# Seven block products for eight in the two feed-forward stages of a hybrid decoder layer, with a replanned order of work

## The chip, the cores and the metric

The kernel runs on all 8 NeuronCores of one Trainium2 chip, one batch element on each, with no traffic between them. The metric is the device time of the slowest core in microseconds. TensorE is written PE, VectorE DVE, ScalarE ACT, GpSimd POOL and SyncE SP.

## The reference, cut to what matters

Each core takes x of shape 2048 x 1024 (tokens x channels) and computes one layer:

```
x = x + 0.5 * swiglu(rmsnorm(x, ffn1_norm), ffn1_w1, ffn1_w3, ffn1_w2)
... two token mixers on rmsnorm(x), gated and merged, then an output projection
... cross-attention to 256 memory tokens
x = x + 0.5 * swiglu(rmsnorm(x, ffn2_norm), ffn2_w1, ffn2_w3, ffn2_w2)
return rmsnorm(x, final_norm)
swiglu(h, w1, w3, w2) = (silu(h @ w1) * (h @ w3)) @ w2
```

w1 and w3 are 1024 x 2816, w2 is 2816 x 1024. The hidden width 2816 is 22 blocks of 128, called m below. Inputs and output are float32.

## The kernel before, in words

**Stages.** In order of time the kernel runs the first feed-forward stage (FFN1), the mixers, their merge and output projection, the cross-attention, and the second feed-forward stage (FFN2). Matmul operands are bf16, sums are float32 in the eight PSUM banks of 128 x 512. Tokens are cut into 4 blocks tb of 512 and 16 tiles tt of 128. hT holds the normalised activations, transposed: channels on the partitions (8 chunks k of 128), tokens along the row.

**Gate and up (FFN.w13, matmuls at L733, a helper that records every group).** For each m and each tb there are two products of 128 hidden units by 512 tokens, one with w1 (the gate) and one with w3 (the up part), each 8 matmuls of 128x128 by 128x512 summed in one bank. Over both products and two token blocks that is 32 matmuls per m and pair of token blocks. ACT takes silu of the one bank into STMP, DVE multiplies it by the other bank into HID (L1031).

**Down (FFN.w2).** The 22 blocks are taken in groups of 6, 6, 5 and 5. After each group, for every token tile and each half of the 1024 output channels, 6 or 5 matmuls sum the group's share in a bank and DVE adds 0.5 times the bank to the resident X (L1049), 4 x 32 additions of 128 x 512 per stage. After the last group FFN1 normalises the tile for the mixers and writes X to DRAM (park); FFN2 does the final norm and writes the output.

**Weights** are loaded by POOL's DMA queue (W<-f_w), cast from float32 to bf16 on the way, into rings of nine slots for w1/w3 and nine for w2. x, parks, rows and transposes by DMA (L940) are on SP's queue. A norm of a tile is a Square with a sum on ACT, a small DVE and a small POOL operation, a product on DVE (HB, L936), and either eight PE transposes with one copy out of the bank (L948, L956) or a DMA transpose.

**Side work in FFN1.** Beside FFN1's matmuls run the rotary tables, the centring of w_v, the small constants, and the jobs on the memory tokens (XW weights, mem_jobs), which are tied to the products in FFN1.

**The order** is not that of the program text. Prog records every operation with its reads, writes and an estimated cost; Prog.schedule plans the order of each engine by list scheduling, priority to the longest remaining path, with 70 ns for each hand-over between engines, 1/300 ns per byte and 2500 ns for a DMA; banks of one class are handed out in the order in which the program asks for them. Each engine then executes its list in order and waits on semaphores. The planning is repeated with the times of the last plan for the DMAs (PASSES).

The softmax here doesn't subtract the row's maximum and nothing guards it: scores larger than these inputs give would overflow.

## Time and profile before

| | us |
|---|---|
| median of the 3 runs shown | 2022.11 |
| lowest and highest of them | 1789.02 and 2107.54 |
| span of the profiled execution (slowest core, core 1) | 1787.4 |
| PE busy | 1707.4 (96%) |
| DVE busy | 876.6 (49%) |
| ACT busy | 648.9 (36%) |
| POOL busy | 374.1 (21%) |

The span runs from the first to the last instruction of the slowest core. The lowest run, 1789.02, stands 1.6 us over it and is what the profiled execution is set beside here; the other two runs are far above it. Busy shares of PE are of matmuls, their ends are modelled. Of the page's 40 slices of the span, PE shows 9 tenths or more in 38.

### The profile page before, as it was taken

How to read it: one execution, taken by the hardware profiler on the slowest of the kernel's cores; microseconds unless marked ns; L12 is line 12 of the kernel's file. 1: busy time of each engine (PE TensorE's matmuls, PEld its weight loads, DVE VectorE, ACT ScalarE, POOL GpSimd, SP SyncE). 2: the span in 40 equal slices, each digit the busy share in tenths (PEclk: the TensorE clock that was granted, in tenths of full speed). 3: DMA queues.
4: the chain of work that ended last, by engine and by line, in shares of the span. 5: the costliest groups of instructions: out<-in, count | busy, mean ns of one | idle time of the engine just before them, and what ended most of it. 6: DMA issues, size and time to landing. Idle time of an engine off the chain costs nothing.

```text
span 1787.4 us, 24179 instructions; the slowest of 8 cores (1769.0 to 1787.4 us)
## 1 busy us (share of the span) xinstructions
PE 1707.4 (96%) x8344; PEld 804.7 (45%) x8344; DVE 876.6 (49%) x1289; ACT 648.9 (36%) x1002; POOL 374.1 (21%) x424
## 2 busy tenths in 40 slices
PE   6999999999999989989999999998999999999997
PEld 4444454444444444444444444443444444444443
DVE  4776523244567746465665433464552232333455
ACT  5411111111236775765677633243431101011122
POOL 2200011100124444343454443210010000000000
PEclk9999999999999999999999999998999999999999
DMA  9845366721973532222112683636170320420022
GB/s 238 152 89 137 100 104 110 129 48 36 177 169 71 119 65 48 50 41 54 37 30 51 137 207 90 175 71 90 36 118 12 59 36 1 71 36 13 13 89 95
DMA packets 98647, 152.09 MB, mean 85 GB/s; under 512 B 48224, under 2 KB 60512, under 8 KB 96480
## 3 DMA queue, kind: packets, MB, share of 16 engines
q0 software_dynamic: 25488, 62.40, 22.4%
q1 hardware_dynamic: 73040, 88.14, 17.0%
q8 instruction: 70, 1.15, 0.3%
q14 instruction: 49, 0.40, 0.1%
HBM read 168.87 MB, written 33.55 MB: 113 GB/s over the span
## 4 chain that ended last, share of the span: by engine, by line
PE 84%; DMA 6%; issue 3%; DVE 3%; ACT 2%; POOL 1%; DVEq 0%; POOLq 0%; ACTq 0%; SPq 0%
PE bank L733 81%; DMA W<-f_w 2%; DMA hT<-HB 1%; DMA XW<-w_xv 1%; DMA XW<-w_xqT 1%; DVE XC L1245 1%; PE bank L948 1%; DVE T L1323 0%; POOL MU L1279 0%; POOL QK L1326 0%; DMA X<-x 0%; ACT L749 0%; DMA XW<-w_xo 0%; DMA out<-OST 0%; DVE XC L1285 0%
## 5 line engine op out<-in xcount | busy, mean ns | idle before, releaser
L733 PE MATMUL bank<-hT,W 128*128 128x512 bf16 (+1 forms) x2880 | 620.7, 376 | 3.1 <-DVE hT L956 3.1
L733 PEld LDWEIGHTS bank<-hT,W 128*128 128x128 bf16 x2880 | 282.8, 98 | 329.8 <-issue 6.1
L749 ACT ACTIVATE STMP<-bank 128x512 f32<-128x512 f32 x176 | 104.9, 596 | 629.5 <-PE bank L733 608.7
L733 PE MATMUL bank<-W,HID 128*128 128x512 bf16 x1408 | 310.6, 379 | 1.4 <-DVE HID L1031 1.4
L1049 DVE SCALAR_TENSOR_TENSOR X<-bank,X 128x512 f32<-128x512 f32 x256 | 175.1, 689 | 202.0 <-PE bank L733 201.0
L1031 DVE TENSOR_TENSOR HID<-bank,STMP 128x512 bf16<-128x512 f32 x176 | 119.8, 689 | 272.2 <-PE bank L733 270.0
L733 PEld LDWEIGHTS bank<-W,HID 128*128 128x128 bf16 x1408 | 137.7, 98 | 165.7 <-issue 1.8
L762 POOL DMA_DIRECT2D W<-f_w x89 | 48.5, 546 | 525.5 <-PE bank L733 447.9
L749 ACT ACTIVATE JUNK<-X 128x1024 bf16<-128x1024 f32 x80 | 84.5, 1056 | 141.7 <-DVE X L1049 63.2
L928 POOL TENSOR_TENSOR stat<-stat,cst 128x1 f32<-128x1 f32 x82 | 49.4, 604 | 367.9 <-DVE stat L927 362.8
L733 PE MATMUL bank<-hT,RW 128*128 128x512 bf16 x512 | 118.4, 382 | 1.6 <-DVE T L1323 0.7
L733 PE MATMUL bank<-hT,GW 128*128 128x512 bf16 x512 | 116.7, 379 | 2.9 <-DVE SC L1375 1.5
L733 PE MATMUL bank<-hT,LW 128*128 128x512 bf16 x512 | 116.2, 382 | 0.5 <-DVE SG L1336 0.5
L936 DVE SCALAR_TENSOR_TENSOR HB<-X,stat,ROW 128x1024 bf16<-128x1024 f32 x64 | 81.9, 1282 | 50.7 <-POOL stat L928 36.4
L1245 DVE SCALAR_TENSOR_TENSOR XC<-XL,pc,XC 128x1024 f32<-128x1024 f32 x48 | 65.5, 1364 | 43.1 <-ACT XL L749 41.4
L1543 DVE SCALAR_TENSOR_TENSOR TT<-TT,bank 128x512 f32<-128x512 f32 x64 | 43.8, 687 | 79.9 <-PE bank L733 75.9
L733 PEld LDWEIGHTS bank<-hT,LW 128*128 128x128 bf16 x512 | 50.3, 98 | 61.8 <-issue 2.9
L733 PEld LDWEIGHTS bank<-hT,RW 128*128 128x128 bf16 x512 | 49.7, 98 | 61.6 <-issue 5.4
L733 PEld LDWEIGHTS bank<-hT,GW 128*128 128x128 bf16 x512 | 49.4, 98 | 60.7 <-issue 4.4
L749 ACT ACT_TABLE_LOAD x50 | 64.2, 1283 | 17.2 <-PE bank L733 10.2
L749 ACT ACTIVATE TT<-GIN,dcol 128x512 f32<-128x512 f16 x64 | 42.8, 714 | 64.8 <-POOL MG L1547 63.2
L733 PE MATMUL bank<-ATP,TW 128*128 128x512 bf16 x256 | 62.1, 387 | 2.7 <-POOL ATP L1458 2.7
(162 smaller groups left out, 1800.5 us busy)
## 6 DMA issues: line engine op xcount, KB each, us to landing
W<-f_w POOLq DMA_DIRECT2D x43, 512.0 KB, 6.0
W<-f_w POOLq DMA_DIRECT2D x46, 256.0 KB, 5.3
X<-x SPq DMA_DIRECT2D x16, 512.0 KB, 7.2
park<-X SPq DMA_DIRECT2D x16, 512.0 KB, 3.0
gate_scr<-GU SPq DMA_DIRECT2D x64, 128.0 KB, 1.9
GIN<-gate_scr SPq DMA_DIRECT2D x8, 1024.0 KB, 6.5
X<-park SPq DMA_DIRECT2D x16, 512.0 KB, 6.2
out<-OST SPq DMA_DIRECT2D x16, 512.0 KB, 2.6
```

The lines of the kernel that those rows point to most:

```text
L733: ins = e.matmul(out_ap, l, r, start=(start and i == 0), stop=(stop and i == n - 1), skip_group_check=skip)
L749: P.add("act", lambda e: e.activation(out, in_, func, **kw), reads=reads, writes=writes, cost=act_cost(n, nap), tab=tab)
L762: P.add("pool", lambda e: e.dma_start(out=out, in_=in_), reads=reads, writes=writes, cost=600, dma=nbytes)
L928: pool(lambda e: e.tensor_tensor(s[:, 2:3], s[:, 1:2], cc(2), ALU.pow), hs + cst.hs, hs, 550)
L936: dve(lambda e: e.scalar_tensor_tensor(hb.ap, src.ap, r, row.ap, ALU.mult, ALU.mult), src.hs + rh + row.hs, hb.hs, D)
L948: ins = e.transpose(bv[:, c * 128:(c + 1) * 128], hb.ap[:, c * 128:(c + 1) * 128], identb.ap)
L1031: dve(lambda e: e.tensor_tensor(hd.ap, banks[b3][:, :], s.ap, ALU.mult), [hbk[b3]] + s.hs, hd.hs, TB)
L1049: dve(lambda e, b=b, xv=xv: e.scalar_tensor_tensor(xv.ap, banks[b][:, :], 0.5, xv.ap, ALU.mult, ALU.add), [hbk[b]] + xv.hs, xv.hs, 512)
L1245: dve(lambda e, s=s: e.scalar_tensor_tensor(xc.ap, XL.v(s, 1024).ap, pcol("conv_w", s * 8 + c), xc.ap, ALU.mult, ALU.add), xl_all.hs + xc. ...
L1543: dve(lambda e, t=t, by=by: e.scalar_tensor_tensor(t.ap, t.ap, 1.0, banks[by][:, :], ALU.add, ALU.mult), t.hs + [hbk[by]], t.hs, TB)
```

## The change

The diff does these things together.

- **Gate and up (FFN.unit)** works on a block of two by two: rows of hT in two halves of 512 channels, and two token blocks of 512; columns of the weights in gate and up. The four 4-matmul half products for each of the four results (8 products of 4 matmuls) are replaced by seven, in the form with sums of blocks: s1, s2, s3, s4 of the activations and t1 to t4 of the weights. All seven are summed in three banks (al, be, ep); bank al is read four times while it is added to. The sums of the activations (FFN.sums) are made by DVE once for each pair of token blocks; those of the weights (FFN.wsum) by DVE for m below 5 and by POOL for the others. Values are rounded to bf16 and stored as fp16, so that sums of them fit. In FFN1 the first five m on the first two token blocks stay plain (FFN.plain).
- **Evacuation**: per unit three copies and two silus on ACT, three additions and one product on DVE, one product on POOL.
- **All 22 m go before the down projection**; HID is held for all tokens, X isn't resident. The down projection sums 22 matmuls in a bank, reloads x (or the park) tile by tile from DRAM, and adds once. Four tiles share the eight banks while w2 arrives (WAVE, CHUNKS).
- **Down of FFN2 (down_blocks)**: after the first four tiles, seven products of 11 matmuls for eight, on pairs of token tiles and halves of the hidden width and of the output.
- **Weights** go through five slots (NSLOT) instead of nine; w2 is loaded whole into space that the gate and up phase gives back.
- **The memory jobs move** from FFN1 into the first five steps of the mixers (MSCHED); two gate pieces are early (EARLY); the rest of the side work stands beside FFN1's down projection.
- **The first loads** are in a written order (ORDER0), at most four under way (WIN0).
- **Attention**: the normalisation of one head's exponentials is recorded after the scores of the next.
- **The last tile** (tt 14, which comes after 15) is finished in halves (last_tile).
- **The planner** gets a latency for each pair of engines, 1/240 ns per byte and 3000 ns for a DMA, and a random addition to the priorities by seeds (SEEDS, JIT).

```diff
-SEM_NS = 70.0
-DMA_NS_PER_B = 1.0 / 300.0
-DMA_LAT = 2500.0
+DMA_NS_PER_B = 1.0 / 240.0
+DMA_LAT = 3000.0
+LAT = {("pe", "act"): 262.0, ("pe", "dve"): 272.0, ("act", "dve"): 140.0, ("dve", "act"): 95.0, ("dve", "pool"): 145.0,
+       ("act", "pool"): 145.0, ("pool", "dve"): 104.0, ("pool", "act"): 95.0}
...
-GROUPS = [6, 6, 5, 5]
...
+NSLOT = 5
+LEAD = 4
+LEAD2 = 3
+TDVE = 5
+NPLAIN = 5
+ORDER0 = "x0 r x1 w0 x2 x3 w1 x4 w2 x5 x6 x7 w3 x8 x9 w4 x10 x11 x12 x13 x14 x15"
+WIN0 = 4
+WAVE = 4
+CHUNKS = [4] + [2] * 9
...
     class FFN:
+        def load13(self, after=((), ())):
...
+            raw = s if direct else WSB[m % NSLOT]
+            for r in range(2):
+                v = raw.v(r * D, D)
+                wdma(v.ap, w13_d[self.which][m][:, r * D:(r + 1) * D], list(after[r]), v.hs, 128 * D * 4)
+            if not direct:
+                v, w = raw.v(0, 2 * D), s.v(0, 2 * D)
+                dve(lambda e: e.tensor_copy(w.ap, v.ap), v.hs, w.hs, 2 * D, 0.27)
+            b12, b22, b11, b21 = (s.v(i * 512, 512) for i in (2, 3, 0, 1))
+            t2, t3, t4 = (s.v(i * 512, 512) for i in (4, 5, 6))
+            self.pend = [(t3, b22, b12), (b12, b12, b11), (t2, b22, b12), (t4, b21, t2)]
...
+        def wsum(self, m, pend=None):
+            for d, x, y in pend or self.pend:
+                f = (lambda e, d=d, x=x, y=y: e.tensor_tensor(d.ap, x.ap, y.ap, ALU.subtract))
+                if m < TDVE:
+                    dve(f, x.hs + y.hs, d.hs, 512, 0.55)
                 else:
+                    pool(f, x.hs + y.hs, d.hs, pool_cost(512))
...
+        def sums(self, p):
+            for d, x, y, op in ((s1, q[2], q[3], ALU.add), (q[2], q[0], q[2], ALU.subtract), (s2, s1, q[0], ALU.subtract),
+                                (s4, q[1], s2, ALU.subtract)):
+                dve(lambda e, d=d, x=x, y=y, op=op: e.tensor_tensor(d.ap, x.ap, y.ap, op), x.hs + y.hs, d.hs, 4 * TB, 0.55)
+        def unit(self, m, p, bk):
...
+            al, be, ep = bk.next(), bk.next(), bk.next()
...
+            prod(al, 0, 0, True)
+            cp(e1)
+            prod(be, 1, 1, True)
+            addb(e1, be)
+            act(e1.ap, e1.ap, AF.Silu, e1.hs, e1.hs, TB, tab=S_SILU)
+            prod(al, 4, -2, False)
+            cp(e2)
+            prod(ep, 5, 2, True)
+            prod(al, 2, -1, False)
+            cp(e4)
+            addb(e4, ep)
+            prod(al, 3, -3, False)
...
+            dve(lambda g: g.tensor_tensor(ha, bv, e1v, ALU.mult), [hbk[al]] + e1.hs, hha, TB)
+            prod(ep, 6, 3, False)
+            addb(e2, ep)
+            act(e2.ap, e2.ap, AF.Silu, e2.hs, e2.hs, TB, tab=S_SILU)
...
+            pool(lambda g: g.tensor_tensor(hb_, e2v, e4v, ALU.mult), e2.hs + e4.hs, hhb, pool_cost(TB))
...
+            for i in range(LEAD2 if self.which else LEAD):
+                go(0)
+            self.sums(1)
+            for m, pend in self.late:
+                self.wsum(m, pend)
+            while done[1] < NM:
+                go(1)
+                if done[0] < NM:
+                    go(0)
+            for m in MORDER:
+                self.load2(m)
...
+        def down_blocks(self, src_d, hsrc, post):
...
+                prod(al, a11, row(W2, 0, 0), True)
+                addx(a, 0, al)
+                prod(be, a12, row(W2, 1, 0), True)
+                addx(a, 0, be)
+                prod(al, s2, tq(0), False)
+                addx(b, 0, al)
+                prod(ep, s3, tq(1), True)
+                addx(b, 1, ep)
+                prod(al, s1, row(W2H, 0, 1), False)
+                addx(b, 1, al)
+                prod(ep, a22h, tq(2), False)
+                addx(b, 0, ep)
+                post(b, vb)
+                prod(al, s4, row(W2H, 1, 1), False)
+                addx(a, 1, al)
+                post(a, va)
```

## Rows read from the trace of the kernel before

**Rows 1.** Spans and mean granted clock, the slowest and the fastest core

```profile
core 1: 1787.4 us, clock 0.986
...
core 4: 1769.0 us, clock 0.994
```

**Rows 2.** Busy time per engine of core 1 (the page's first part), PE's line

```profile
PE 1707.4 (96%) x8344; PEld 804.7 (45%) x8344; DVE 876.6 (49%) x1289; ACT 648.9 (36%) x1002; POOL 374.1 (21%) x424
```

**Rows 3.** Stretches of core 1: from:to, length, busy us (instructions) per engine, clock, DMA share, GB/s

```profile
0.00:28.00 28.00, 10.69 (x80) 7.71 (x80) 12.25 (x29) 14.80 (x24) 7.94 (x20) 1.00 0.92 225
28.00:240.00 212.00, 211.92 (x1118) 106.11 (x1119) 130.71 (x253) 56.61 (x91) 27.18 (x50) 0.99 0.59 128
240.00:340.00 100.00, 94.51 (x501) 48.39 (x500) 27.68 (x41) 18.90 (x34) 15.82 (x30) 0.99 0.70 118
...
520.00:1020.00 500.00, 471.00 (x2384) 226.15 (x2382) 308.00 (x388) 338.23 (x488) 215.17 (x170) 0.99 0.30 66
...
1206.00:1232.00 26.00, 17.08 (x76) 7.46 (x75) 10.47 (x11) 7.86 (x14) 2.64 (x4) 0.88 1.02 137
...
1340.00:1760.00 420.00, 420.00 (x1948) 190.38 (x1947) 150.69 (x224) 61.56 (x104) 19.77 (x37) 1.00 0.18 39
1760.00:1787.40 27.40, 14.72 (x68) 6.31 (x66) 13.18 (x19) 5.79 (x10) 2.74 (x5) 0.84 0.24 97
```

**Rows 4.** Waits of PE over the span: waiter, releaser, us, times, longest

```profile
PE bank L948 <- DVE HB L936: 14.5, 4, 11.8
PE bank L733 <- ACT PEX L749: 9.8, 2, 8.9
...
PE bank L733 <- DMA XW<-w_xo: 2.3, 1, 2.3
```

**Rows 5.** Groups of instructions by shape: count, busy us, mean ns, idle before them

```profile
L733 PE MATMUL bank<-hT,W 128*128 128x512 bf16 x2752 | 602.8, 379 | 0.0
```

**Rows 6.** Timeline: start, us, what; PE's last matmul to ACT, and ACT to PE

```profile
1209.91 0.59 PE L733 MATMUL bank<-PEX,onesb 128*128 128x512 bf16 x2
...
1210.60 0.60 ACT L749 ACTIVATE RI<-bank 128x512 f32<-128x512 f32 x1 [1.51 <-PE bank L733]
...
1228.81 1.26 ACT L749 ACTIVATE PEX<-bank 128x512 bf16<-128x512 f32 x2
...
1230.21 1.01 PE L733 MATMUL bank<-PEX,onesb 128*128 128x512 bf16 x2 [8.92 <-ACT PEX L749]
```

**Rows 7.** Groups by shape, as above, for ACT, DVE and POOL

```profile
L749 ACT ACTIVATE STMP<-bank 128x512 f32<-128x512 f32 x176 | 104.9, 596 | 629.5 <-PE bank L733 608.7 <-DVE HID L1031 17.9 <-DVE WVM L878 2.9
...
L1049 DVE SCALAR_TENSOR_TENSOR X<-bank,X 128x512 f32<-128x512 f32 x256 | 175.1, 689 | 202.0 <-PE bank L733 201.0 <-issue 0.6
L1031 DVE TENSOR_TENSOR HID<-bank,STMP 128x512 bf16<-128x512 f32 x176 | 119.8, 689 | 272.2 <-PE bank L733 270.0 <-ACT RT L749 1.6
...
L894 DVE TENSOR_TENSOR RT<-RT 128x512 f32<-128x512 f32 x12 | 8.2, 688 | 0.6
...
L1394 DVE COPY KT<-bank 128x512 bf16<-128x512 bf16 x14 | 5.8, 417 | 9.7 <-PE bank L1388 9.5
...
L762 POOL DMA_DIRECT2D W<-f_w x89 | 48.5, 546 | 525.5 <-PE bank L733 447.9 <-DMA W<-f_w 57.1 <-DMA XW<-w_xqT 8.4
L1326 POOL TENSOR_TENSOR QK<-T 128x512 bf16<-128x512 f32 x32 | 46.5, 1452 | 62.3 <-DVE T L1323 59.6 <-PE bank L733 2.4
...
L1547 POOL TENSOR_TENSOR MG<-TT 128x512 bf16<-128x512 f32 x32 | 40.5, 1265 | 67.4 <-DVE TT L1543 67.3
```

**Rows 8.** DMA issues: count, KB each, median us from issue to landing

```profile
W<-f_w POOLq DMA_DIRECT2D x46, 256.0 KB, 5.3
...
X<-x SPq DMA_DIRECT2D x16, 512.0 KB, 7.2
```

**Rows 9.** Timeline of the end: the last down matmuls and the last final product

```profile
1767.29 8.79 PE L733 MATMUL bank<-W,HID 128*128 128x512 bf16 x40 [1.37 <-DVE HID L1031]
...
1780.25 1.28 DVE L967 SCALAR_TENSOR_TENSOR OST<-X,stat,ROW 128x1024 f32<-128x1024 f32 x1 [0.92 <-DMA out<-OST]
```

More of the change, by code:

```diff
@@ L304, in schedule @@
                 s.nd -= 1
[L305 to L307 removed]
+                w = end + lat(op, s.eng)
+                if w > s.ready:
+                    s.ready = w
                 if s.nd == 0:
@@ new lines, in __init__ @@
+            self.n13 = 0
+            self.units = 0
+            self.late = []
+        def load13(self, after=((), ())):
+            m = self.n13
+            self.n13 += 1
+            s = WS[m % NSLOT]
+            direct = self.which == 0 and m < TDVE
+            raw = s if direct else WSB[m % NSLOT]
[8 more added lines that the diff above has]
+            self.pend = [(t3, b22, b12), (b12, b12, b11), (t2, b22, b12), (t4, b21, t2)]
+            if self.which or m >= NPLAIN:
+                self.wsum(m)
+            else:
+                self.late.append((m, self.pend))
@@ new lines, in up, with go @@
+        def up(self, side=()):
+            bk = Banks(P, 2)
+            side = list(side)
+            npl = NPLAIN if self.which == 0 else 0
+            for t in range(2):
+                for m in range(npl):
+                    self.plain(m, t, bk)
+            self.sums(0)
+            done = [0, 0]
+            def go(p):
+                m = done[p]
+                while self.n13 <= m:
+                    self.load13()
+                if p or m >= npl:
+                    self.unit(m, p, bk)
+                done[p] += 1
+                if p == 1 and self.n13 < NM:
+                    self.load13()
+            for i in range(LEAD2 if self.which else LEAD):
[9 more added lines that the diff above has]
+                self.load2(m)
@@ L1627, in xattn @@
                 scores(tb + 1)
+            else:
+                flush()
             outp(tb)
@@ L1716, in record @@
-    outs = [o for o in P.ops if o.dma and o.eng == "sp"]
+    f1.down(x_d, None, post1, side)
+    ret_load(0)
+    stA, stG, stB = lru_stages()
+    qk, gate_, block = ret_steps()
+    stA(0)
+    stG(0)
+    steps = []
+    for p in range(2):
+        for tb in range(NTB):
+            i = p * NTB + tb
+            nxt = divmod(i + 1, NTB) if i < 7 else None
+            steps.append([lambda p=p, tb=tb: block(p, 2 * tb)])
+            steps.append([lambda p=p, tb=tb: block(p, 2 * tb + 1)])
+            if nxt:
+                steps[-2].append(lambda n=nxt: qk(*n))
+                steps[-1].append(lambda n=nxt: gate_(*n))
@@ new lines, in record @@
+    qk(0, 0)
+    gate_(0, 0)
+    gp = gate_piece()
+    pieces = [(oc, br) for oc in range(KC) for br in range(2)]
+    for i in range(EARLY):
+        gp(*pieces.pop(0), 3 + i)
+    mj = mem_jobs([])
+    assert sum(GSCHED) + EARLY == 16
+    for u in range(16):
+        if u + 1 < 16:
+            stA(u + 1)
+        stB(u)
+        if u == RWU:
+            ret_load(1, BT[u // 2].v((u % 2) * 1024, 1024).hs)
+        for f in steps[u]:
+            f()
+        for i in range(GSCHED[u]):
+            gp(*pieces.pop(0), 0 if u < 8 else 1 if u < 12 else 2)
+        for i in range(MSCHED[u]):
+            mj.pop(0)()
+        if u + 1 < 16:
+            stG(u + 1)
@@ L1717, in record, with post2, pump @@
+    assert not mj
+    tail()
+    f2 = FFN(1)
+    rowf = load_row("ffn2_norm", NF)
+    def post2(tt):
+        norm_x(NF, xt(tt), tt, rowf, None if tt < TR3 else bkT)
+        park(xt(tt), tt)
+    def pump(n):
+        for i in range(3):
+            f2.load13()
+    xattn(post2, pump)
+    f2.up()
+    fr = load_row("final_norm", NE)
+    f2.down_blocks(park_d, h_park, lambda tt, v: final_tile(v, tt, fr))
+    act(warm.ap[:, 0:1], identb.ap[:, 0:1], AF.Square, identb.hs, warm.hs, 1)
     last = P.add("sp", None, reads=[], writes=[h_out])
-    for o in outs[-16:]:
+    for o in out_ops:
```

654 lines of the change are left out of this document (387 added, 267 removed).

## The prediction

> **What bounds the kernel now.** I read the spans and clocks of the cores first. The slowest core is 18.4 us longer than the fastest, and both have a granted clock of nearly 1 [rows 1], so the time is that of dense 2.4 GHz matmuls. The sum below is made against the profiled execution: span 1787.4, and 1789.0 with what lies around it. The median of the three runs, 2022.11, is 13% above it; I forecast the time that stands beside 1789.0, not one beside 2022. Next the busy times: PE 1707.4 of 1787.4, no other engine over half [rows 2]. PE's idle time is 80 us. Then the stretches [rows 3]: in the middle of FFN2 (1340 to 1760) PE is busy all 420.0 us with 1947 weight loads, so one 128x128 by 128x512 matmul costs 420.0/1947 = 215.7 ns and nothing else costs anything. The idle time lies elsewhere: 17.3 us in the first 28, 5.5 us beside the memory jobs (240 to 340), 29 us in the mixers (520 to 1020), 8.9 us in one wait at 1206 to 1232, and some 11 us after the last matmul. The waits of PE name the first (a normalised tile), the one at 1230 (exponentials that stood behind a late tile of hT) and small ones for XW weights [rows 4]. So two feed-forward stages are bound by the number of matmuls, and that number is what the change alters.
>
> **Products.** Both stages have 22 m and 2 pairs of token blocks. Gate and up of one stage: 44 x 32 = 1408 matmuls before; the idle before them is nil [rows 5]. After, a unit has 7 x 4 = 28. FFN2: 44 x 4 = 176 fewer. FFN1: five m of the first pair stay plain, 39 x 4 = 156 fewer. Down of FFN2: six pairs of tiles, each 7 x 11 = 77 for 88, 66 fewer. Together 398 x 0.2157 = **85.8 us** less. The plain ones are issued as halves of 256 columns; the kernel before does so for part of them, I add 0.4 us for the rest.
>
> No fp16 matmul is in this trace. From below such a matmul can't be under 215.7 ns, since the 512 columns stream at the top clock already; from above the nearest row is PE at its lower clock, 2 matmuls in 1.01 us beside 0.59 us [rows 6]. I take 215.7: an fp16 operand is as wide as a bf16 one. The Trainium skill, "FP8 and Floating Point Precision" (TensorE Precision Notes), says both are widened to the same internal format; no run here shows it yet.
>
> **What the seven products cost the other engines, per unit of 28 matmuls (6.04 us of PE).** ACT: three copies out of a bank and two silus, 5 x 0.596 [rows 7] = 2.98 us. DVE: three additions and one product with a bank, 4 x 0.689 = 2.76, and half a conversion of 2048 weights: from 0.35 (four elements in the time of one) to 0.83 (KT's rate, 417 ns for 512), so 3.1 to 3.6. POOL, per m, two units, 12.08 us of PE: four subtractions and two products of 512, at 1265 to 1452 ns, and two DMA issues at 546: 8.7 to 9.8 us. All are under PE's time, POOL by 2.3 us at worst. Against this the down additions fall from 256 to 32 + 8 + 42 = 82, 174 x 0.689 = 120 us less of DVE, worth nothing in time since PE never waited for them [rows 5]. Sums of activations: 16 operations of 2048, 1.3 us each at the copy rate to 2.4 at RT's (688 ns for 512), once per pair. All hidden but the ones at the start.
>
> **The turn of bank al.** It is read and added to again. From PE's last matmul to ACT's start is 1210.60 - 1210.50 = 0.10, the copy 0.60, from ACT's end to PE 0.14 [rows 6]: 0.84 us, up to 1.0 if ACT is busy with a silu. The product between (be or ep) is 4 x 0.2157 = 0.86 us and covers it just; the third turn has nothing between, but the tail of the neighbouring unit can stand there, as two units need 6 of 8 banks. Bounds: 0 and 83 x 1.0 = 83 us. I take 6 us, near 0, since the order is planned with these latencies.
>
> **Weights.** With five slots and a lead of four m, slot m is released near the end of a unit and its next content is wanted 12.1 us and a third of a unit later, 14 us. It takes 0.55 issue, 5.3 landing [rows 8], 0.7 to 1.7 conversion, three subtractions 3.8 to 4.4, hops 0.5: 10.9 to 12.5 us, plus a POOL product in the way. It fits by about 1 us in FFN1; in FFN2 the lead is three and it fits by 12 more. Nothing in the sum. Behind POOL's wait for the slot stand its own products for HID, which the down needs much later.
>
> **Start.** The first 28 us stay as they are: first tile, first weight, one norm. Then the old order had 12 x 2 plain products on half the tokens; the new one has 10, 160 x 0.2157 = 34.5 us, with some 11 us of transposes: PE's work ends near 17.3 + 46 = 63 us. The last x tile lands after 8.4 + 0.5 + 2.6 = 11.5 MB at 225 GB/s [rows 3], 51 us (the old X loads took 7.2 each, queued), then 5 us of norm and 5 to 9 of sums: 61 to 65. I add 2 us (0 to 10).
>
> **Up to down, down to mixers.** Eight w2 rows can land before the last unit; the wave takes 8 matmuls, 1.7 us, per row against 0.5 MB. Mixer buffers come free only with the last down tile, where before they came earlier. I add 3 us (-2 to 12).
>
> **Memory jobs.** Their 5.5 us of waits leave FFN1; in the mixers, where ACT is busy 68% and DVE 62%, I give 3 back: -2.5. Their matmuls move with them, which costs nothing. But extra independent matmuls beside the chains of the mixers, and latencies nearer to those of [rows 6] in the plan, should fill part of 29 us idle: -5 (-18 to +12). POOL's and SP's queues carry 40 more issues there.
>
> **Cross-attention.** The 8.9 us wait was a DMA transpose late behind the ring loads for FFN2; fewer loads fit now. It hit core 1, not all cores: -4 (0 to -9). The FFN2 start: three units, 18 us, cover the last tile's norm, transpose and sums, some 15 us; 0.
>
> **End.** From PE's last matmul, 1767.29 + 8.79 = 1776.1, to 1787.4 are 11.3 us, in which DVE worked off additions for four banks, and the last product started at 1780.25 [rows 9]. Now two additions, half squares, half products and half DMAs: about 7 us. -4 (-6 to 0).
>
> **Sum:** 1789.0 - 85.8 + 0.4 + 6 + 2 + 3 - 2.5 - 5 - 4 - 4 = **1699 us**.
>
> **Rivals.**
> 1. *The turn isn't covered.* If units don't interleave, each pays 0.84 to 1.0 us for its third turn: 83 x 0.92 = 76 us for 6: 1769, no change by the 2% bound. For it: three banks and strict order of first use keep the next unit from starting before this one's fourth product. Against it: four products of the neighbour remain to fill with. It decides from 60 us of turns.
> 2. *POOL becomes the bound, slower than before.* Place: the weight sums of m 5 to 21 in both stages, 34 m. POOL's time per m is 1.1 + 6 x TT; PE's is 12.08, so it decides from TT = 1.83 us; it ends over 1825 from (1825 - 1699)/34 = 3.7 us more per m, TT = 2.46. At 2.6 us: 1699 + 34 x 4.6 = 1855. For it: the same shape already takes 1265 ns in one stretch and 1452 in another where DVE is busier, and DVE will be at half load with two-input operations beside it. Against: that spread is 15%, and 95% more is needed. The Trainium skill, "SBUF — State Buffer" (Practical consequences), has a rule that speaks against this change: a DVE instruction with two SBUF inputs, or in a two-port mode, and a POOL instruction lock each other out for a whole instruction. The trace agrees in direction only. By it POOL would lose the conversion and little else per m, since the bank operations have one SBUF input; the time would stay 1699, and I give the rival 2 of its 5 in 100 for it.
> 3. *Other stages take it back.* Start, hand-overs and mixers at the bad ends of their bounds (+8, +9, +17): 1733, still faster by over 2%, inside the range.
> 4. *More comes free.* Mixers -18, attention -9, start 0, turns 0: 1673.
> 5. *fp16 runs as slow as PE's lower clock:* 1800 such matmuls at 0.2 us more, over 2000 us. 1 in 100.
>
> **Chances.** A change of this kernel can be told from none beyond about 2%, below 1753 or above 1825. My sum with rivals 3 and 4: 85 in 100, all faster. Rival 1: 9, of which 8 the same and 1 faster. Rival 2: 5, of which 4 slower and 1 the same. Rival 5: 1. Faster 0.86, same 0.09, slower 0.05. The range is 1670 (all good ends of the small terms) to 1742 (rival 3 with a few us of turns more); what lies beyond is most of rivals 1, 2 and 5, and 3 or so at either side.
>
> **What would show it.** PE's matmul count should fall by about 400, with the mean of an fp16 and a bf16 matmul alike. The middle of gate and up in both stages should show PE at 98% or more; idle before `al` products released by ACT would be rival 1. POOL's subtractions should show at 1.3 to 1.45 us; PE waiting for POOL or for the DVE conversion would be rival 2. The granted clock should be 1 there: gaps of under 1 us didn't lower it before, the 8.9 us gap did, 0.88 [rows 3]. XW waits should stand in the mixers; from last matmul to end about 7 us. I'm wrong if the matmul count falls and the feed-forward stages don't shorten by about 50 (FFN2) and 33 us.

## The result, and the profile after

| us | before | after |
|---|---|---|
| median of all runs | 1789.02 | 1689.62 |
| lowest to highest | 1785.97 to 2107.54 | 1685.73 to 1966.48 |
| span, slowest and fastest core | 1787.4, 1769.0 | 1688.1, 1672.5 |
| PE busy on the slowest core | 1707.4 | 1608.5 |

In some executions a few cores run at a lower granted clock and take longer; the ratio is of the runs without that, 0.9445, 95% interval 0.943 to 0.946: 99 us, or 5.5%, faster. Forecast were 1699 us in a range of 1670 to 1742.

The cores of the kernel after are again at a clock of nearly 1, as in [rows 1]:

```profile
core 0: 1688.1 us, clock 0.992
...
core 7: 1672.5 us, clock 0.995
```

The busy times of core 0, beside [rows 2]: PE lost 99 us, ACT gained 133, DVE 118 and POOL 301, and none of them is over 60%. The PEld column holds the weight loads, one for each matmul; it is the safer count, as about 100 matmul records are missing in this trace. (Before, PE shows 9 tenths or more in 35 of the page's 40 slices, not in 38.)

```profile
PE 1608.5 (95%) x7955; PEld 774.5 (46%) x8058; DVE 994.4 (59%) x1480; ACT 781.7 (46%) x1247; POOL 675.5 (40%) x687
```

The loads fall by 286, from 8344 to 8058, and that is the forecast count: 398 matmuls fewer, 96 more because a plain matmul issued in halves of 256 columns is counted twice (160 for 64 of them), and 16 more transposes on PE.

Stretches of core 0 (columns as in [rows 3]):

```profile
0.00:20.00 20.00, 2.63 (x20) 1.99 (x21) 4.63 (x14) 5.84 (x9) 5.21 (x14) 1.00 0.91 202
20.00:40.00 20.00, 15.95 (x122) 12.51 (x120) 6.80 (x11) 6.64 (x11) 3.65 (x7) 0.91 0.95 206
40.00:60.00 20.00, 16.18 (x168) 14.04 (x166) 17.75 (x28) 11.86 (x20) 3.85 (x7) 1.00 0.65 174
...
160.00:300.00 140.00, 139.97 (x649) 63.27 (x648) 73.17 (x103) 67.84 (x116) 93.33 (x94) 1.00 0.34 52
...
460.00:480.00 20.00, 12.07 (x49) 5.08 (x49) 12.04 (x16) 8.04 (x13) 4.90 (x6) 0.83 1.02 203
480.00:500.00 20.00, 17.39 (x92) 8.29 (x92) 11.59 (x14) 11.26 (x14) 7.28 (x6) 1.00 0.68 129
500.00:520.00 20.00, 14.49 (x59) 5.93 (x58) 10.83 (x16) 7.22 (x13) 5.55 (x6) 0.91 0.58 157
...
1300.00:1500.00 200.00, 200.00 (x928) 90.58 (x927) 104.17 (x154) 97.03 (x167) 137.92 (x133) 1.00 0.29 46
```

What to see: in gate and up of both stages PE is busy all the time (139.97 of 140, 200.00 of 200), at 200.00/927 = 215.7 ns for a matmul, as before. POOL's share there is 67 to 69%. The idle time stands at two places: 21.4 us in the first 40 with 3.8 more up to 60, and 16.1 us from 460 to 520, where FFN1 hands over to the mixers.

Groups by shape (columns as in [rows 5]) of the new work:

```profile
L795 PE MATMUL bank<-hTh,WS 128*128 128x512 f16 x1328 | 314.8, 379 | 1.3 <-DVE WS L1092 1.1
L795 PE MATMUL bank<-SUM,WS 128*128 128x512 f16 x996 | 243.3, 379 | 2.7 <-ACT EV L811 2.0 <-DVE SUM L1119 0.7
...
L1103 POOL TENSOR_TENSOR WS<-WS 128x512 f16<-128x512 f16 x136 | 158.4, 1166 | 28.3 <-DVE WS L1092 17.8 <-PE bank L795 0.8 <-ACT EV L811 0.4
...
L1178 POOL TENSOR_TENSOR HID<-EV,EV 128x512 bf16<-128x512 f32 x83 | 106.0, 1282 | 67.7 <-ACT EV L811 62.6 <-PE bank L795 4.2
...
L1092 DVE CAST WS<-WSB 128x2048 f16<-128x2048 bf16 x39 | 34.6, 886 | 10.1 <-DMA WSB<-f_w 10.1
```

An fp16 matmul takes 379 ns by the profile, the same as the bf16 one of [rows 5]. PE's idle time ahead of the products with summed activations, where the turn of bank al would show, is 2.7 us over 996 matmuls. PE's waits (columns as in [rows 4]); the first is the start, and the old wait for exponentials is gone:

```profile
PE bank L1019 <- DVE n1HB L1003: 19.6, 6, 16.2
PE bank L795 <- POOL XCB L1550: 10.1, 3, 7.9
PE bank L795 <- DMA RW<-w_g: 5.2, 1, 5.2
...
PE bank L795 <- ACT EV L811: 2.0, 2, 1.2
```

How the turn is covered shows in the timeline (columns as in [rows 6]). The two copies out of a bank, 0.60 us each on ACT, run beside PE's matmuls, and no idle time stands in brackets behind any PE line:

```profile
179.81 1.67 PE L795 MATMUL bank<-SUM,WS 128*128 128x512 f16 x7
...
180.72 0.60 ACT L811 ACTIVATE EV<-bank 128x512 f32<-128x512 f32 x1 [0.99 <-PE bank L795]
...
181.32 1.03 PE L795 MATMUL bank<-hTh,WS 128*128 128x512 f16 x4
...
181.58 0.60 ACT L811 ACTIVATE EV<-bank 128x512 f32<-128x512 f32 x1 [0.27 <-PE bank L795]
```

**By stage.** The boundaries are the last down matmul of FFN1, the first matmul of the mixers' merge, the last of the attention and the last of all. The slowest core of each profiled run:

| us | FFN1 | mixers | merge, attention | FFN2 | end | sum |
|---|---|---|---|---|---|---|
| before | 528.5 | 464.5 | 325.7 | 457.4 | 11.3 | 1787.4 |
| after | 464.5 | 501.1 | 306.9 | 406.3 | 9.3 | 1688.1 |
| difference | -64.0 | +36.6 | -18.8 | -51.1 | -2.0 | -99.3 |
| difference of the medians of the 8 cores | -65.2 | +34.8 | -6.2 | -51.7 | -2.1 | -90.4 |

Cores of one run differ by up to 18 us: before mostly in merge and attention (323 to 326 us on cores 1, 3 and 7, 310 to 313 on the others), after in the mixers (488 to 501; merge and attention take 306.9 on all eight). So some 8 of the 99 us are a wait that only three cores had, and on the median core the kernel gained 91.

### The profile page after: what moved, and what is told of

Its sections match the earlier page's. It is cut to its first block, busy times and chain, and to the rows that moved or that the text cites. A ratio compares the mean times of both kernels' runs of the same rounds, so it can differ in the third digit from the quotient of the medians.

```text
span 1688.1 us, 24738 instructions; the slowest of 8 cores (1672.5 to 1688.1 us)
## 1 busy us (share of the span) xinstructions
PE 1608.5 (95%) x7955; PEld 774.5 (46%) x8058; DVE 994.4 (59%) x1480; ACT 781.7 (46%) x1247; POOL 675.5 (40%) x687
## 4 chain that ended last, share of the span: by engine, by line
PE 86%; DVE 4%; DMA 4%; issue 3%; ACT 1%; POOL 1%; POOLq 0%; DVEq 0%; ACTq 0%
PE bank L795 83%; DMA W<-f_w 1%; DMA RW<-w_g 1%; DVE XC L1543 1%; DMA WS<-f_w 1%; PE bank L1019 1%; DMA XW<-w_xqT 1%; DVE n1HB L1003 0%; DMA LW<-w_lru_in 0%; PE bank L1716 0%; PE bank L1719 0%; DVE SUM L1119 0%; PE bank L1748 0%; DVE T L1625 0%; DVE XC L1585 0%
## 5 line engine op out<-in xcount | busy, mean ns | idle before, releaser
L795 PE MATMUL bank<-hTh,WS 128*128 128x512 f16 (+1 forms) x1648 | 355.6, 361 | 2.2 <-DVE WS L1092 1.1
L1148 DVE TENSOR_TENSOR EV<-bank,EV 128x512 f32<-128x512 f32 x249 | 169.1, 689 | 188.6 <-ACT EV L811 106.5
L795 PE MATMUL bank<-SUM,WS 128*128 128x512 f16 x996 | 243.3, 379 | 2.7 <-ACT EV L811 2.0
L795 PEld LDWEIGHTS bank<-hTh,WS 128*128 128x128 f16 x1648 | 162.1, 99 | 165.2 <-issue 4.7
L795 PE MATMUL bank<-W,HID 128*128 128x512 bf16 x987 | 218.7, 379 | 1.7 <-DMA W<-f_w 0.3
L811 ACT ACTIVATE EV<-bank 128x512 f32<-128x512 f32 x259 | 152.0, 593 | 125.4 <-PE bank L795 117.9
L811 ACT ACTIVATE EV<-EV 128x512 f32<-128x512 f32 x166 | 104.0, 628 | 161.7 <-DVE EV L1148 161.6
L1103 POOL TENSOR_TENSOR WS<-WS 128x512 f16<-128x512 f16 x136 | 158.4, 1166 | 28.3 <-DVE WS L1092 17.8
L795 PEld LDWEIGHTS bank<-SUM,WS 128*128 128x128 f16 x996 | 97.0, 98 | 121.2 <-issue 5.5
L1178 POOL TENSOR_TENSOR HID<-EV,EV 128x512 bf16<-128x512 f32 x83 | 106.0, 1282 | 67.7 <-ACT EV L811 62.6
```

Source lines behind the costliest of these rows:

```text
L795: ins = e.matmul(out_ap, l, r, start=(start and i == 0), stop=(stop and i == n - 1), skip_group_check=skip)
L811: P.add("act", lambda e: e.activation(out, in_, func, **kw), reads=reads, writes=writes, cost=act_cost(n, nap), tab=tab)
L1103: f = (lambda e, d=d, x=x, y=y: e.tensor_tensor(d.ap, x.ap, y.ap, ALU.subtract))
L1148: dve(lambda g: g.tensor_tensor(e.ap, banks[bank][:, :], e.ap, ALU.add), [hbk[bank]] + e.hs, e.hs, TB)
L1178: pool(lambda g: g.tensor_tensor(hb_, e2v, e4v, ALU.mult), e2.hs + e4.hs, hhb, pool_cost(TB))
```

## The experiments

All ratios are to the kernel before of the same runs. The theory: the products are worth what the matmul count says, the other engines and the turn are hidden, and the rest is small terms. The rivals: the turn, POOL, and an order of work that earns or costs more than I gave it.

### How much is the order, how much the products?

**e1.** The kernel after, with the random additions to the priorities set to nothing.

```diff
-JIT = 3000.0
+JIT = 0.0
```

> The changed kernel with the random addition to the planner's priorities set to zero; the same operations, another order. If the gain is the 398 matmuls and the order is a detail worth some 5 us (the prediction's term for the mixers), it takes 1690 to 1700 us. If the order found by the seeds carries much of the gain, it takes 1720 us or more, with the difference in PE's idle time at the start, the hand-over to the mixers and in the mixers, and the dense middle of gate and up unchanged.

Measured: 1743.55 us, ratio 0.9741 (0.9718 to 0.9765): 54 us of the 99 hang on the seeds. Stages on its slowest core: 467.5, 551.7, 303.4, 409.0, 9.4. So the feed-forward stages hardly need the seeds (3 us each), and the mixers lose 50.6 us by their absence.

**e2.** The same, and gate, up and the second down with eight products again; new stage order, reloads, moved memory jobs stay.

```diff
 # FFN.up
-                    self.unit(m, p, bk)
+                    self.plain8(m, 2 * p, bk)
+                    self.plain8(m, 2 * p + 1, bk)
...
-    f2.down_blocks(park_d, h_park, ...)
+    f2.down(park_d, h_park, ...)
-LASTH = True
-JIT = 3000.0
+LASTH = False
+JIT = 0.0
```

> As e1, but gate and up with eight products per unit (two banks per token block and m, silu and one product out of the bank) and the down projection of FFN2 plain, the last tile whole: 398 matmuls more than e1, no sums, no POOL subtractions, everything else (memory jobs moved, full hidden width held, weights through five slots) as changed. If each matmul saved is worth 215.7 ns in full, it is 80 to 88 us over e1. If units pay for turns or for POOL, it is less than 75 us over e1. It also tells what everything but the products brings: e1's order, no block products, against the kernel before at 1789.

Measured: 1815.97 us, ratio 1.0146 (1.0116 to 1.0175). Beside e1 the products are worth 72.4 us, where the count gives 85.8. Stages 507.2, 527.3, 316.6, 455.8, 7.9: FFN1 gives 39.7 and FFN2 46.8 for the products, 86.5 together, while the mixers, whose order differs, take 24.4 more in e1 and merge and attention 13.2 less. So under 75 us, which I had tied to turns or POOL, came about by the order of other stages. The 39.7 hold 6.9 us of idle time that e2 has more in FFN1 (36.8 against 29.9), and in FFN2 e1 idles some 3.5 us more: without these the products give 32.8 and 50.3, for 33.6 and 52.2 by the count.

**e9.** The question from the other side: the kernel before, with the change's planner and seeds chosen for it.

```diff
-SEM_NS = 70.0
-DMA_NS_PER_B = 1.0 / 300.0
-DMA_LAT = 2500.0
+DMA_NS_PER_B = 1.0 / 240.0
+DMA_LAT = 3000.0
+LAT = {...}                       # as in the change, used in schedule
-PASSES = 3
+PASSES = 1                        # as in the change; the plan is made again once, not three times
+SEEDS = [0, 0, 261, 261, ...]     # 120, chosen for this kernel
+JIT = 3000.0
+                op.key += JIT * rnd[seed of op.jid][op.jid]
```

> The kernel before with its eight products, its groups of down and its memory jobs in FFN1; only the planner is changed: the latencies of the change and random priorities in 120 pieces, chosen for this kernel over some hundreds of plans. It asks whether what the seeds earn (54 us by e1) is theirs alone or needs the changed stages. Theory A, a badly ordered stage is what seeds repair: the kernel before has only some 60 us of idle outside the end and the start, 29 of it in the mixers, and its mixers with merge and attention took 790 us against 808 in the kernel after; I expect -8 to -25 us, 1765 to 1781, ratio 0.986 to 0.995, with the mixers and merge shorter by most of it. Theory B, seeds are a gain of their own in any kernel of this size: about -50 us, 1740, ratio 0.972. Theory C, the kernel before was as well ordered as it gets: 1785 to 1792, ratio 0.998 to 1.002.

**e10.** The same without SEEDS and JIT: the latencies alone.

> The kernel before, with nothing but the planner's latencies, bank hand-over time and DMA speed of the change, no random priorities. With e9 it splits the planner's part in two. Theory A, the latencies nearer to the measured hops make the order better by itself: the waits of 5.5 us by the memory jobs and part of the 29 us in the mixers go, 1775 to 1785. Theory B, they alone do nothing, as PE idles only 80 us and its longest waits were a norm at the start and a late transpose by DMA: 1786 to 1794, ratio 0.998 to 1.003, and all of e9's gain is the seeds'.

Measured: e9 1749.91 us, ratio 0.9778 (0.9755 to 0.98); e10 1779.75, ratio 0.9941 (0.992 to 0.9962). The latencies are worth 0.6%, 10 us, and the seeds 1.6%, 29 us, with eight products. (e10 keeps PASSES = 3, so the 29 us are those of the seeds together with PASSES = 1; no run parts the two.) e9 lies between my theories A and B: A was too low and its ground was wrong, as I counted only PE's idle time. e10 is in the range of its theory A, but not where I looked for it: its mixers idle more than before, not less, as the first two lines here show. The stretches of the mixers, in turn of the kernel before, e10, e9, e1 and after (the columns are those of [rows 3]):

```profile
529.00:993.00 464.00, 436.63 (x2199) 208.66 (x2198) 287.72 (x356) 312.96 (x453) 195.52 (x150) 0.99 0.26 57
```

```profile
526.00:1005.00 479.00, 445.26 (x2242) 212.38 (x2241) 303.08 (x367) 315.26 (x457) 215.80 (x154) 0.98 0.28 58
```

```profile
528.00:964.00 436.00, 420.05 (x2157) 204.75 (x2155) 287.90 (x352) 306.31 (x440) 199.63 (x150) 1.00 0.30 65
```

```profile
467.00:1019.00 552.00, 486.75 (x2508) 238.24 (x2506) 318.27 (x394) 338.05 (x493) 221.42 (x183) 0.96 0.41 83
```

```profile
464.00:966.00 502.00, 464.21 (x2406) 233.20 (x2452) 317.79 (x385) 322.54 (x477) 211.90 (x183) 0.98 0.45 90
```

PE's idle time there is 27.4, 33.7, 16.0, 65.3 and 37.8 us. PE's busy time per weight load is 199, 199, 195 ns in the first three, and 194 and 189 ns in the last two: with gaps the granted clock falls (0.99, 0.98, 1.00, 0.96, 0.98), and the matmuls that remain take longer. From e1 to after 27.5 us are idle time and 22.5 busy time, of which 2506 loads at 5 ns, 12 us, go with the clock and the rest are 54 matmuls that after does behind the boundary, in the merge. A better order pays twice.

### The latencies and the attention

My step for the 8.9 us wait named a late transpose and put -4 us to the space that the rings give back. Merge and attention took 325.7 us before and 306.9 after; e10 changes nothing but the planner's constants, and there they take 302.9. Its stretch beside that of the kernel before:

```profile
993.00:1319.00 326.00, 309.98 (x1476) 142.66 (x1475) 155.73 (x224) 136.73 (x216) 84.52 (x96) 0.97 0.54 118
```

```profile
1005.00:1308.00 303.00, 299.79 (x1452) 138.75 (x1451) 150.10 (x216) 129.96 (x210) 78.94 (x96) 1.00 0.56 126
```

The idle time falls from 16.0 to 3.2 us, and the clock goes from 0.97 to 1.00, with all rings of weights as they were: the gain doesn't need ring space. But it is smaller than the 22.8 us between the two stages: 24 loads more stand ahead of the boundary in e10, whose mixers take 14.3 us longer (478.8 against 464.5). And the constants don't bring it about by themselves: e2 has them, the deferral and the freed space, and idles 11.4 us in this stage, which takes 316.6. The late transpose is in one plan and not in another; what decides it stays open.

**e11** prices the deferral of the attention's normalisation.

```diff
-                wait.append(norm)
+                norm()
-JIT = 3000.0
+JIT = 0.0
```

> The kernel after without random priorities (as e1), with the normalisation of one head's exponentials recorded at once, not after the scores of the next head. Beside e1 (1743.55, ratio 0.9741; merge with attention 303.4 us on its core) it prices the deferral. Theory A, the deferral is what shortened the merge and attention (325.7 us before, 303 to 307 after): 310 to 322 us there, the time +8 to +18, 1752 to 1761, ratio 0.979 to 0.984. Theory B, the shortening is the space that the rings of weights gave back, so that the transposes by DMA came in time: within 4 us of e1, ratio 0.972 to 0.977.

Measured: 1747.55 us, ratio 0.977 (0.9749 to 0.979), merge and attention 303.1 us against 303.4 in e1. The deferral does nothing in that stage. The time is 4.0 us over e1, within theory B, and the interval of the ratio overlaps that of e1. Theory B's reason, the ring space, is what e10 speaks against.

### The turn of the bank, and the overlap of units

**e3.** At most three banks for gate and up's units, so that two units can't hold banks at once except as one gives them back.

```diff
-            bk = Banks(P, 2)
+            bk = Banks(P, 2, 3)
```

> The changed kernel with at most three banks for gate and up, so that a unit can start only when the one before gives its banks back. My account: the turn of bank al is 0.84 to 1.0 us and hidden only by the neighbouring unit; without that each of 83 units pays 0.8 to 1.5 us, 65 to 125 us more than 1690. Rival (the turns are covered inside a unit anyway): under 20 us more.

Measured: 1758.02 us, ratio 0.9817 (0.9789 to 0.9845). Gate and up take 5 us more in FFN1 and 10 in FFN2 than in e1; from 160 to 300 PE is busy 139.13 of 140. The total, 68 us over after, lies in my 65 to 125 by chance: 53 of it are outside the feed-forward stages (mixers +38.3, merge and attention +14.5), where a changed plan no longer fits the seeds. For the turn my account was wrong: with PE busy so fully, three banks don't separate the units. The next one can take up a bank as soon as this one's last read of it is through.

**e5.** Separates them truly: the first product of a unit waits for the HID of the unit before.

```diff
-            prod(al, 0, 0, True)
+            prod(al, 0, 0, True, self.prevh)   # reads HID of the last unit, for the order alone
...
             ha, hha = hid(a)
+            self.prevh = hha
```

> The changed kernel, each unit of gate and up made to wait until the unit before has given bank al back (its first product also waits for the product of al into HID). My price of the turn: the third turn is bare, 0.84 to 1.0 us, the first two leave at most 0.14 each, and the hand-over of al to the next unit is 0.1 + 0.69 + 0.15 against a product of 0.86: 1.1 to 1.5 us per unit, 83 units, 90 to 125 us over 1690. Rival 1's price of 0.92 per unit would give 76. Rival (turns are cheap by themselves): under 30.

Measured: 1893.87 us, ratio 1.0577 (1.0553 to 1.0601), 204 us over after; I had expected 90 to 125. Stages on its slowest core: 541.6, 526.5, 311.3, 503.3, 9.3. So the units in series cost 77.1 in FFN1 and 97.0 in FFN2, 174 us or 174/83 = 2.1 per unit; the other 30 stand in the mixers and the merge, which hold no unit. PE's largest wait, and a piece of the timeline:

```profile
PE bank L795 <- ACT EV L811: 127.3, 147, 2.0
```

```profile
201.42 1.03 PE L795 MATMUL bank<-SUM,WS 128*128 128x512 f16 x4
...
202.54 0.60 ACT L811 ACTIVATE EV<-bank 128x512 f32<-128x512 f32 x1 [0.16 <-PE bank L795]
...
203.28 1.02 PE L795 MATMUL bank<-SUM,WS 128*128 128x512 f16 x4 [0.84 <-ACT EV L811]
...
205.14 1.02 PE L795 MATMUL bank<-SUM,WS 128*128 128x512 f16 x4 [0.84 <-ACT EV L811]
...
206.00 3.86 PE L795 MATMUL bank<-hTh,WS 128*128 128x512 f16 x16
```

The bare turn leaves PE idle for 0.84 us, as the hops of [rows 6] said, and costs 1.0: the products start 1.86 us apart (201.42, 203.28, 205.14), where four matmuls in a row take 0.86. And it comes bare 147 times in 83 units, nearly twice in each, not once: the four products with plain activations, one of which could stand in the first turn, are done in one row of 16 matmuls. 147 turns at 1.0 us are most of the 174. Overlap of units is what hides them: in after PE's wait for these copies is 2.0 us in all.

### POOL

**e4.** Eight subtractions for four in each weight sum on POOL (some written again with the same value).

```diff
-                    pool(f, x.hs + y.hs, d.hs, pool_cost(512))
+                    for _ in range(n_times):   # 2, 1, 3, 2: eight in all, the plan as if four
+                        pool(f, x.hs + y.hs, d.hs, pool_cost(512))
```

> The changed kernel with eight subtractions of weights per m on POOL for four (each result is computed again, the values stay). POOL's time per m becomes 2 x 0.61 + 8 x 1.17 + 2 x 1.28 = 13.1 us for 12.08 of PE. If POOL is bound by its busy time alone, 34 m cost 1.0 us each: 1720 to 1730. If its waits in order (for a slot, for a silu) already use the slack, 3 us or more per m: 1790 or more. If it stays within 5 us of 1690, POOL had more slack than worked out.

Measured: 1783.3 us, ratio 0.9965 (0.9947 to 0.9983), 94 us over after: 37.7 in FFN1 and 49.1 in FFN2. The stretch that answers to 160 to 300 above, and PE's waits:

```profile
160.00:300.00 140.00, 123.13 (x541) 51.69 (x539) 70.00 (x88) 56.34 (x97) 123.73 (x116) 0.98 0.26 36
```

```profile
PE bank L795 <- DVE WS L1092: 24.9, 8, 7.6
...
PE bank L795 <- POOL WS L1103: 11.2, 10, 2.1
```

The two stages lose 86.8 us, 34 m times 2.6 us, between my two expectations (1.0, and 3 or more). POOL is busy 88%, and PE's largest new waits are for the weights: for the conversion, whose load POOL issues, and for POOL's own subtractions, 36 us together. So the mechanism of rival 2 is real, and POOL stands one third of its time away from it: with 1166 ns for a subtraction it is at 67%; with twice the subtractions it holds PE up though it isn't at 100%.

### The smaller parts

**e6.** The second down projection with eight products.

```diff
-    f2.down_blocks(park_d, h_park, lambda tt, v: final_tile(v, tt, fr))
+    f2.down(park_d, h_park, lambda tt, v: final_tile(v, tt, fr))
-LASTH = True
+LASTH = False
```

> The changed kernel with FFN2's down projection plain, 22 matmuls per half tile, last tile whole; all before it is the same. The sum says 66 x 0.2157 = 14.2 us more, plus 1 to 3 for the last tile. If DVE, which has some 12 us of work per pair of tiles in 16.6 of PE, or the conversion of w2 had eaten part of the gain, it is under 10 us more.

Measured: 1714.31 us, ratio 0.9573 (0.9554 to 0.9592). In the profiled run cores 4 and 5 took 1712.7 and 1707.1 us at a clock of 0.977, the other six 1687.5 to 1696.5, so FFN2 is read by itself: it takes 418.9 us on all eight cores, against 406.3 on the slowest of after (12.6 more) and 405.7 on the median core (13.2 more), for 66 matmuls, 14.2 by the count.

**e7.** Three first loads under way at once instead of four.

```diff
-WIN0 = 4
+WIN0 = 3
```

> The changed kernel with at most three of the first loads under way for four, so that the first weights wait for the first x tile. In the changed kernel the row of the norm lands late and PE's first transpose starts at 16.2 us for 11.8 before; if the two weight loads issued at 1.6 us cause that, the first transpose moves to 12 to 13 us and 2 to 4 us are won. If the last x tile sets the start (63 us by the sum), nothing is won, or 1 to 3 us are lost, since fewer loads are under way.

Measured: 1707.59 us, ratio 0.9508 (0.9427 to 0.9589), too wide to tell; the profiled cores had 1675 to 1690 us, against 1672 to 1688 in after, and PE idles 21.7 us in the first 40, as against 21.4. Nothing is won.

**e8.** The memory jobs left out (M and V of the memory are a constant), no random priorities.

```diff
-    mj = mem_jobs([])
+    mj = []          # and one constant tile stored in place of their results
-JIT = 3000.0
+JIT = 0.0
```

> As e1 (no random addition), with the memory jobs in the mixers left out: the attention reads constants in place of the two products of the memory tokens. They hold 192 matmuls of 256 columns and 32 of 512, and two transposed tiles, some 28.9 us of PE. If they cost the mixers their matmuls alone: 29 us less than e1, 1715. If they fill idle time of the mixers, as the prediction has it: 24 us less or fewer. If they disturb the chains of the mixers (their evacuations, their weights' loads): 35 us less or more, under 1709.

Measured: 1707.92 us, ratio 0.9469 (0.9442 to 0.9497); cores 4 and 5 were at a clock of 0.966 here too, the median core took 1691 us against 1738 in e1. So the jobs cost 47 us in all. Their matmuls are 128 and 64 of 256 columns, 32 of 512 and 16 transposes, at 108, 216 and 57 ns some 29 us. The other 18 us are a net of the plan, without seeds: on core 0 the mixers are 68 us shorter than in e1 (485.1 against 553.2), while merge and attention take 17 more and the end 2 more. It is disturbance, as the last of my three cases had it, but not in the mixers alone.

**e12.** The last tile finished whole.

```diff
-LASTH = True
+LASTH = False
```

> The kernel after with the last tile finished whole instead of in halves; seeds, waves and all else as in the change. It prices the last part of the change. My step for the end held -4 us for it together with the fewer additions; 11.3 us before, 9.3 after from the last matmul to the end. Theory A, the halves are worth what the last operations take less: half a square, half a product and half a DMA, some 1 to 1.5 us: 1689.8 to 1691.5, ratio 0.945 to 0.946, end 10.3 to 11 us. Theory B, halves add operations and an extra statistic (0.87 us on POOL) on the chain and gain nothing: 1687 to 1690, end 8.5 to 9.5 us. Either is near what three rounds can tell; the end of the trace is read for it, on the core that ends last and on others.

Measured: 1687.4 us, ratio 0.9431 (0.9411 to 0.9452), not told from after by its interval. But the end can be read off: from PE's last matmul to the end of the span it is 7.8 to 8.0 us on all eight cores, and 9.2 to 9.4 on all eight of after. The end of after's core 0 (its span ends at 1688.1), with the three last issues of output transfers by SP:

```profile
1676.26 2.54 PE L795 MATMUL bank<-W2H,DS 128*128 128x512 f16 x11
...
1680.89 0.33 SPq L821 DMA_DIRECT2D out<-OST  x1
...
1682.04 0.72 ACT L811 ACTIVATE OST<-OST,stat 128x512 f32<-128x512 f32 x1 [1.58 <-POOL stat L1050]
...
1683.64 0.33 SPq L821 DMA_DIRECT2D out<-OST  x1
...
1685.77 0.33 SPq L821 DMA_DIRECT2D out<-OST  x1
```

The same of e12 (its span ends at 1683.6), whose last matmul ends at 1675.72:

```profile
1677.94 0.33 SPq L821 DMA_DIRECT2D out<-OST  x1
...
1678.89 1.28 DVE L1063 SCALAR_TENSOR_TENSOR OST<-XR,stat,neROW 128x1024 f32<-128x1024 f32 x1 [0.88 <-POOL stat L994]
...
1680.68 0.33 SPq L821 DMA_DIRECT2D out<-OST  x1
```

The transfers of after from 1676 on: count, KB each, median us from issue to landing:

```profile
out<-OST SPq DMA_DIRECT2D x1, 512.0 KB, 2.6
out<-OST SPq DMA_DIRECT2D x2, 256.0 KB, 2.0
```

Theory B, and more: the halves cost 1.4 us, which neither theory had. In halves the arithmetic ends sooner after the last matmul: 1682.76 - 1678.80 = 3.96 us against 1680.17 - 1675.72 = 4.45. But it isn't what ends last. Both halves are ready by 1682.76, and SP issues them at 1683.64 and 1685.77, each 0.12 us after the transfer before it has landed. That is the kernel's own doing: all output transfers write one handle (h_out), so the planner makes each of them wait for the one before. In e12 the whole tile is ready at 1680.17 and issued at 1680.68, after the transfer before it. In this chain one transfer of 512 KB takes 2.6 us, and two of 256 KB take 2 x 2.0 and a hand-over of 0.12. Halving adds one link to a chain that was already the bound, and saves arithmetic that wasn't.

## Why the prediction was right, and what it had wrong

The sign and the likeliest case were right, and the number 9 us short of a gain of 99. In parts, against the profiled spans of the slowest cores (forecast for a stage is the sum of its terms; the 29 us of memory matmuls, which the prediction moved at no cost, are put out of one stage and into the other):

| us | forecast | measured |
|---|---|---|
| FFN1 | -33.6 products, -29 and -5.5 memory jobs, +2 start, +3 turns: -63 | -64.0 |
| mixers, merge, attention | +29 +3 memory jobs, +2 hand-over, -5 order, -4 attention: +25 | +17.8 |
| FFN2 | -52.2 products, +3 turns, +1 hand-over: -48 | -51.1 |
| end | -4 | -2.0 |

**Products.** 398 matmuls were predicted, at 215.7 ns whether bf16 or fp16; the profile shows both. FFN2 came out at -51.1 (-51.7 on the median core) for a count of -52.2; e2 against e1, without the idle time that differs, has 50.3 there, and 32.8 in FFN1 for a count of 33.6. Holding this for the main term was right.

**The turn.** Predicted 6 us, found 2 by PE's waits. The cover is the overlap of units, as said. But rival 1 was priced wrong. I took one bare turn of 0.92 us per unit, 76 us, and from it no change by the 2% bound. e5 shows that units in series cost 174 us in the two stages, nearly two turns of 1.0 us in each: slower than before. It also names the condition wrong: three banks alone don't bring it about (e3).

**POOL.** The subtraction came out at 1.17 us, below both rows it was bounded by, and POOL at 67%: right. Rival 2's deciding point was too late. By its sum POOL has 1.1 + 8 x 1.17 + 2 x 1.28 = 13.0 us of work per m in e4, 0.9 over PE's 12.08; measured are 2.6 over, with POOL at 88%. That its work comes in pieces that wait for the conversion, and so binds before it is at 100%, fits but wasn't tested apart.

**The port rule.** The DVE conversion of 2048 elements takes 0.69 us in the last line here, and longer in the two where POOL works (timeline of after, as above):

```profile
177.72 0.60 POOL L824 DMA_DIRECT2D WSB<-f_w  x1
177.95 2.11 DVE L1092 CAST WS<-WSB 128x2048 f16<-128x2048 bf16 x1
178.34 1.17 POOL L1103 TENSOR_TENSOR WS<-WS 128x512 f16<-128x512 f16 x1
...
186.61 2.51 POOL L1178 TENSOR_TENSOR HID<-EV,EV 128x512 bf16<-128x512 f32 x2 [0.21 <-ACT EV L811]
187.64 0.69 DVE L1148 TENSOR_TENSOR EV<-bank,EV 128x512 f32<-128x512 f32 x1 [1.04 <-PE bank L795]
188.68 0.98 DVE L1092 CAST WS<-WSB 128x2048 f16<-128x2048 bf16 x1 [0.35 <-DMA WSB<-f_w]
...
214.63 0.69 DVE L1092 CAST WS<-WSB 128x2048 f16<-128x2048 bf16 x1 [1.20 <-DMA WSB<-f_w]
```

POOL was already at work when each of the two began, and they end 0.55 and 0.54 us after the POOL instruction that ran beside them. The addition with one operand in a bank keeps its 0.69 us beside the same POOL instruction. The Trainium skill, "SBUF — State Buffer" (Practical consequences), has a rule for this: a DVE instruction in a two-port mode, such as a conversion can have, and one of GpSimd shut each other out, and the one that comes second waits for the whole of the first. The trace agrees: it is the conversion, begun second, that was held up, and POOL kept its 1.17. Over the run a conversion takes 0.89 us in the mean.

**Start.** Predicted +2; PE idles 27.1 us up to 88, against 17.4 before in the same stretch, so nearly +10, the bad end. Four to six of it are there in e9 and e10 as well (21.4 and 23.0 us in the first 40, 17.4 before; 21.4 in after): they come with the planner's new constants, and the new load order isn't needed for them. FFN1 still came out as forecast, as some 6 us less stand against it. Most of these are at its boundary: before, 17 matmuls of the mixers stand ahead of the last down matmul, after only one, 3.5 us; and PE does 128 transposes in FFN1 for 144, 0.9 us. Some 2 us stay open.

**Up to down, and the hand-over.** Predicted +3 for both. The hand-over shows 16.1 us of idle time from 460 to 520, with a wait for XCB and one for a gate weight (RW) in the list of waits. Before, the same place had about 4. That it is the mixers' loads and buffers that come only with the last down tile fits (DMA share 1.02 from 460 to 480) but wasn't tested.

**The failed step: "Memory jobs".** It gave the jobs' disturbance 3 us and the better order 5. Without seeds the new stages cost far more: e2 takes 36 us more than e10 (eight products and the same latencies in both, new and old stages, PASSES 1 and 3): 62 more in mixers and attention, 29 of them the moved matmuls, against some 25 less elsewhere. With seeds the order gives 54 back. I had put one small term, -5 (-18 to +12), where two large ones of opposite sign stood. The total was right partly because they cancel, and that is luck.

**Attention.** -4 (0 to -9) for a wait that hit some cores; it was -18.8 on the slowest core, where that wait and 7 us more of idle time went, and -6.2 on the median core. The freed space isn't needed for it (e10), and the deferral does nothing (e11); another order removes the wait, as in e10 and e1, but not every order with the new constants does (e2).

**End.** Forecast 7 us from the last matmul; 9.3 measured, 7.9 without the halves. The new down projection gave 3.4 us (11.3 to 7.9), and the halves took 1.4 back. I had put the 11.3 us to DVE's additions and left out the output transfers. Before, the last three are issued 2.76 us apart (1777.44, 1780.20 and 1782.96), each when the one before has landed, and even DVE's last product waits for one of them (the [0.92 <-DMA out<-OST] of [rows 9]). That chain is there before and after, and a handle of its own for each tile would loosen it; no run tried that.

**The ledger**, by ratios to the kernel before: latencies -10 us, seeds (with PASSES = 1) on the old stages -29, both together -39 (e9), and by subtraction all the rest, products with all that they need, -60, for 85.8 us of matmuls. The planner's part needs no change of the arithmetic. What stays open: how the 29 us part between seeds and PASSES, what decides the late transpose, and how much a still better order of the mixers would add to the -60. No version beat the kernel after by more than its runs can tell; e12 is 2 us under it.

## What to carry to other kernels

Where PE is busy 100% of a stage, price a cut in its work by count times the measured matmul, and check each helper engine against its own bound per step; that part is reliable. Price the order of the rest apart, with the one-sided experiment of giving the old kernel the new planner: here that alone was worth 39 us, and without its seeds the whole change some 45 instead of 99. Before cutting the last operations up, look which wait ends last there: here it was a chain of output transfers that the kernel had tied together itself. An idle gap costs its length and a lower clock for the matmuls around it, so a stage with gaps has more to win than its idle time.

## What was unexpected of the hardware

- The clock in the mixers went with the gaps: 1.00 with 16 us idle in 436 (e9), 0.98 with 38 in 502 (after), 0.96 with 65 in 552 (e1), each on the slowest core. But idle time alone doesn't set it. Of e8, the same stretch on core 5 and on core 0:

```profile
466.00:951.00 485.00, 447.22 (x2108) 207.88 (x2107) 284.27 (x351) 294.44 (x423) 181.72 (x141) 0.90 0.33 69
```

```profile
466.00:951.00 485.00, 441.51 (x2189) 212.41 (x2230) 294.19 (x364) 310.70 (x452) 196.05 (x151) 0.97 0.34 72
```

  Core 5, one of the two with a clock of 0.966 over the whole run, idles 38 us there at 0.90, and a load takes 212 ns of PE's busy time; core 0 idles 43 at 0.97 and needs 198 ns. One kernel, one stretch, two clocks: what lowered that of core 5 isn't in the trace.
- A subtraction of 128 x 512 in fp16 on POOL takes 1166 ns, less than its two-input operations on float32 (1265 and 1452 in [rows 7], 1282 for HID here).
- Half the bytes are far from half the time: at the end of after an output transfer of 512 KB takes 2.6 us from issue to landing, one of 256 KB 2.0.
- DVE converts 2048 elements from bf16 to fp16 in 0.69 us beside no POOL work.
